# Five weight places and three key places in a two-layer kernel, with a 4 KB descriptor area

## The reference

```python
def peer(h, wq, subkeys, u_tab, v_tab):
    t = h.reshape(-1, D_MODEL)
    q = (t @ wq).reshape(-1, PEER_HEADS, 2, PEER_QDIM // 2)
    s = jnp.einsum('thpd,hpkd->thpk', q, subkeys)
    sv, si = lax.top_k(s, PEER_TOPK)
    cand = sv[:, :, 0, :, None] + sv[:, :, 1, None, :]
    cv, ci = lax.top_k(cand.reshape(*cand.shape[:2], 256), PEER_TOPK)
    idx = i1 * PEER_KEYS + i2          # the two halves' keys of ci
    g = softmax(cv)
    act = gelu(einsum('td,thkd->thk', t, u_tab[idx]))
    out = einsum('thk,thkd->td', g * act, v_tab[idx])
```

## Time and profile before

| what | value |
|---|---|
| time, median of 3 runs | 2362.88 us (2361.84 to 2364.53) |
| profiled execution: span from its first to its last instruction | 2360.1 us |
| that execution's own time | its span is all that is given; the median stands 2.8 us above it |
| opening, to the first gather | 0 to 176.0 us |
| stages 0 and 1, gathers 0 to 511 | 176.0 to 1586.3 us |
| gap, to gather 512 | 1586.3 to 1664.2 us |
| stage 2, to the last landing and the output | 1664.2 to 2360.1 us |
| DMA, mean over the span | 398 GB/s, 939.43 MB |

### The profile page before, as it was taken

One profiled execution on the slowest core, in us unless ns is written; L12 is line 12 of the kernel. 1 busy time (PEld: TensorE's weight loads), 2 busy tenths in 40 slices (PEclk: granted clock), 3 DMA queues, 4 the chain that ended last, 5 costly groups with the idle time before them and its releaser, 6 DMA issues.

```text
span 2360.1 us, 24134 instructions
## 1 busy us (share of the span) xinstructions
PE 2079.7 (88%) x6896; PEld 1123.8 (48%) x6896; DVE 1609.6 (68%) x3952; ACT 953.4 (40%) x2791; POOL 1019.5 (43%) x868
## 2 busy tenths in 40 slices
PE   8998998899998988988898998798899988777787
PEld 7775554455564434544454544346455533222222
DVE  3855668967766568788866677855765887666454
ACT  2014434543334444444454333534543444444333
POOL 0004444344334444444444454530333555566774
PEclk9999999999999999999999999999999999999999
DMA  9979999999999999999999999996799999999997
GB/s 400 375 291 382 395 399 421 407 421 421 421 420 421 415 421 404 421 421 417 391 421 421 421 421 421 416 370 254 284 365 379 415 421 421 422 421 421 422 421 318
DMA packets 132595, 939.43 MB, mean 398 GB/s; under 512 B 14720, under 2 KB 17920, under 8 KB 18944
## 3 DMA queue, kind: packets, MB, share of 16 engines
q0 software_dynamic: 110592, 805.36, 82.8%
q1 hardware_dynamic: 21888, 132.68, 13.8%
HBM read 936.93 MB, written 1.05 MB: 397 GB/s over the span
## 4 chain that ended last, share of the span: by engine, by line
PE 36%; DMA 33%; DVE 13%; issue 7%; POOL 6%; ACT 5%; POOLq 0%; SPq 0%; DVEq 0%; ACTq 0%
DMA uv<-uv_dram,stage_idx 31%; PE psum L983 19%; PE psum L786 9%; DVE uv L1593 6%; POOL uv L1050 5%; PE psum L768 4%; PE psum L926 1%; DMA uv<-in_dram 1%; ACT diag L1225 1%; DMA uv<-ada_dram 1%; ACT wv L1223 1%; DVE h L1282 1%; PE psum L704 1%; PE psum L957 1%; ACT gel L1221 1%
## 5 line engine op out<-in xcount | busy, mean ns | idle before, releaser
L983 PE MATMUL psum<-uv,diag 128*128 128x512 f32 x3072 | 1447.1, 611 | 227.8 <-ACT diag L1225 217.6
L1050 POOL DMA_INDIRECT uv<-uv_dram,stage_idx x768 | 985.9, 1284 | 1052.3 <-PE psum L983 829.5
L1593 DVE CUSTOM_DVE_ANT_0 uv<-uv,h 128x1024 f32<-128x1024 f32 x768 | 935.1, 1226 | 554.6 <-DMA uv<-uv_dram,stage_idx 545.2
L983 PEld LDWEIGHTS psum<-uv,diag 128*128 128x128 f32 x3072 | 562.1, 192 | 1006.5 <-issue 505.3
L1221 ACT ACTIVATE gel<-dots 128x1 f32<-128x1 f32 x768 | 155.3, 202 | 1060.6 <-DVE dots L1593 1059.7
L1225 ACT ACTIVATE diag<-const,wv 128x128 f32<-128x128 f32 x768 | 308.3, 401 | 25.0
L786 PE MATMUL psum<-hT,wring 128*128 128x256 f32 (+1 forms) x1312 | 273.0, 361 | 0.7 <-ACT hT L1091 0.7
L786 PEld LDWEIGHTS psum<-hT,wring 128*128 128x128 f32 x1312 | 233.1, 190 | 60.2 <-issue 33.0
L1223 ACT ACTIVATE wv<-gel,gw 128x1 f32<-128x1 f32 x768 | 226.3, 295 | 25.0
L1038 POOL COPY stage_idx<-idx 128x8 uint32 (+1 forms) x96 | 33.4, 348 | 265.4 <-DVE idx L1564 264.7
L1073 ACT ACTIVATE work<-psum 128x256 f32<-128x256 f32 (+2 forms) x123 | 47.7, 389 | 128.5 <-PE psum L786 102.1
(11 more groups left out here) (224 smaller groups left out, 1289.8 us busy)
## 6 DMA issues: line engine op xcount, KB each, us to landing
uv<-ada_dram SPq DMA_DIRECT2D x30, 1024.0 KB, 15.8
wring<-in_dram SPq DMA_DIRECT2D x25, 1024.0 KB, 9.5
wring<-wq_dram SPq DMA_DIRECT2D x24, 1024.0 KB, 11.2
uv<-uv_dram,stage_idx POOLq DMA_INDIRECT x768, 14.2
uv<-in_dram SPq DMA_DIRECT2D x9, 1024.0 KB, 13.5
uv<-ada_t_dram SPq DMA_DIRECT2D x7, 1024.0 KB, 22.7
wring<-ada_dram SPq DMA_DIRECT2D x6, 1024.0 KB, 11.2
wring<-ada_t_dram SPq DMA_DIRECT2D x5, 1024.0 KB, 20.7
```

What stands on the lines that cost most here:

```text
L983: last = mm(acc[:, b, :], diag[:, s % RING, :], uv[:, s % RING, D + 512 * b:D + 512 * (b + 1)], start=(c == 0), stop=(c == NSEL - 1))
L1050: nc.gpsimd.indirect_dma_start(out=uv[:, s, :], out_offset=None, in_=tables[stage // 2], in_offset=bass.IndirectOffsetOnAxis(ap=stage_idx[ ...
L1593: v.tensor_tensor_reduce(out=uv[:, r, 0:D], in0=uv[:, r, 0:D], in1=h2[:, row_of[stage], t, :], scale=1.0, scalar=0.0, op0=ALU.mult, op1=AL ...
```

## The change

`WRING` goes from 3 to 5 and the keys' places from 2 to 3 (`KEYS`). The room comes from a smaller area in which GpSimd keeps the descriptors of its DMAs (`dynamic_dma_scratch_size=4096`), from 6 places for the diagonal matrices instead of 8 (`DIAGS`; ACT now waits until PE has used the one six slots back), from `sp_t` laid over the end of `xn`, and from small tiles packed into one. Gap blocks get `uv` slots alone, unless they are used beyond the gap's search, when they get own places. The `out_w` blocks of the opening may lie in `uv` slots 2 to 7 instead of 4 to 7. Head 1's query weights of stage 2 are loaded once. Keys are loaded one query block later than before, except for a stage's first three heads and at its end.

```diff
-WRING = 3
+WRING = 5
-LAST_SLOTS = (4, 5, 6, 7)
+LAST_SLOTS = (2, 3, 4, 5, 6, 7)
 RING = 8
+DIAGS = 6
 LAG = 2
+SCRATCH = 4096
+KEYS = 3
...
-            uses = [(("query", *args[:2], args[3] if reloaded(*args[:2]) else 0), ("wq", args[0] // 2, args[1]))]
+            uses = [(("query", *args[:2], 0), ("wq", args[0] // 2, args[1]))]
...
-    own, opening, gap = list(range(WRING)), list(range(WRING + RING)), list(range(WRING)) + [WRING + i for i in GAP_SLOTS]
+    own, opening, gap = list(range(WRING)), list(range(WRING + RING)), [WRING + i for i in GAP_SLOTS]
...
-        keys = sb("keys", [P, 2, SUB_W])
+        keys = sb("keys", [P, KEYS, SUB_W])
...
-        diag = sb("diag", [P, RING, P])
+        diag = sb("diag", [P, DIAGS, P])
...
+        sp_t = view(work, 2 * D - P, P)
...
-                pe.wait_ge(keys_landed[h % 2], 16 * (stage * PH // 2 + h // 2 + 1))
+                pe.wait_ge(keys_landed[(k - 1) % KEYS], 16 * ((k - 1) // KEYS + 1))
...
-                    last = mm(acc[:, b, :], diag[:, s % RING, :], uv[:, s % RING, D + 512 * b:D + 512 * (b + 1)],
+                    last = mm(acc[:, b, :], diag[:, s % DIAGS, :], uv[:, s % RING, D + 512 * b:D + 512 * (b + 1)],
...
+            def load_keys(layer):
+
+                nonlocal heads
+                heads += 1
+                if heads > KEYS:
+                    sp.wait_ge(*scored[heads - KEYS])
+                sp.dma_start(keys[:, (heads - 1) % KEYS, :], A["keys"][layer, (heads - 1) % PH])\
+                    .then_inc(keys_landed[(heads - 1) % KEYS], 16)
...
-                if kind == "wq" and b == heads % PH:
-                    heads += 1
-                    if heads > 2:
-                        sp.wait_ge(*scored[heads - 2])
-                    sp.dma_start(keys[:, b % 2, :], A["keys"][layer, b]).then_inc(keys_landed[b % 2], 16)
+                if kind == "wq":
+                    queries += 1
+                    while heads < queries and (heads < queries - 1 or queries % PH <= KEYS):
+                        load_keys(layer)
...
-                f(diag[:, r, :], C("ident"), ACT.Copy, scale=wv[:, r:r + 1]).then_inc(diag_ready, 1)
+                if s >= DIAGS:
+                    act.wait_ge(uv_used, RING + s - DIAGS + 1)
+                f(diag[:, s % DIAGS, :], C("ident"), ACT.Copy, scale=wv[:, r:r + 1]).then_inc(diag_ready, 1)
...
-    nc = bacc.Bacc("TRN2", target_bir_lowering=False, num_devices=1)
+    nc = bacc.Bacc("TRN2", target_bir_lowering=False, num_devices=1, dynamic_dma_scratch_size=SCRATCH)
```

More of the change, by code:

```diff
@@ L339, in weight_blocks @@
     return list(blocks.values())
-def reloaded(stage, h):
-    return stage == 2 and h == 1
 def weight_places(program, blocks):
-    own, opening, gap = list(range(WRING)), list(range(WRING + RING)), list(range(WRING)) + [WRING + i for i in GAP_SLOTS]
+    own, opening, gap = list(range(WRING)), list(range(WRING + RING)), [WRING + i for i in GAP_SLOTS]
     found = program.index(("step", ("find", 2, 0, (0,), FIND_PARTS - 1)))
@@ L397, in build @@
         wring = sb("wring", [P, WRING, BLK_W])
-        keys = sb("keys", [P, 2, SUB_W])
+        keys = sb("keys", [P, KEYS, SUB_W])
         hT = sb("hT", [P, KC, TOK])
         h2 = sb("h2", [P, 2, TT, D])
[L402 to L406, removed]
+        small = sb("small", [P, 9 * 2 + 3 * HEADS + 3 * RING + 8])
+        ss_x, ms_x, rr_x, ss_v, ms_v, rr_v, lam_dot, lam_exp, neg_lam = (small[:, 2 * i:2 * i + 2] for i in range(9))
+        ss_o, ms_o, rr_o = (small[:, 18 + HEADS * i:18 + HEADS * (i + 1)] for i in range(3))
+        dots, gel, wv = (small[:, 30 + RING * i:30 + RING * (i + 1)] for i in range(3))
+        unused = small[:, 30 + 3 * RING:38 + 3 * RING]
         ss_heads, ms_heads, root_heads = (sb(s, [P, 16]) for s in ("ss_heads", "ms_heads", "root_heads"))
@@ L416, in build @@
         stage_idx = sb("stage_idx", [P, 2, RING], U32)
-        dots, gel, wv = (sb(s, [P, RING]) for s in ("dots", "gel", "wv"))
         work = sb("work", [P, 8704])
@@ L536, in build @@
         w_landed = [sem(f"w_landed{i}") for i in range(WRING + RING)]
-        keys_landed = [sem(f"keys_landed{i}") for i in range(2)]
+        keys_landed = [sem(f"keys_landed{i}") for i in range(KEYS)]
         act_bank_full, act_took = sem("act_bank_full"), sem("act_took")
@@ L942, in query @@
             def query(stage, h, q, tiles):
-                again = reloaded(stage, h)
-                channel_major(to_act, ("query", h), q, tiles, again or tiles[0] == 0, again or tiles[-1] == TT - 1)
+                channel_major(to_act, ("query", h), q, tiles, tiles[0] == 0, tiles[-1] == TT - 1)
                 n["qh", stage, h] = to_act.n
@@ L956, in score @@
                         o = (q * len(tiles) + i) * P
-                        last = mm(bank[:, o:o + P], qh[:, h % 2, q, t * P:(t + 1) * P], keys[:, h % 2, q * PK:(q + 1) * PK],
+                        last = mm(bank[:, o:o + P], qh[:, h % 2, q, t * P:(t + 1) * P], keys[:, (k - 1) % KEYS, q * PK:(q + 1) * PK],
                                   start=True, stop=True)
@@ L994, in _ @@
             sp.dma_start(const[:, 0:W_EARLY], A["const"][:, 0:W_EARLY]).then_inc(const_loaded, 16)
-            heads = 0
+            heads = queries = 0
+            def load_keys(layer):
[5 more added lines that the diff above has]
+                    .then_inc(keys_landed[(heads - 1) % KEYS], 16)
             for n, (kind, layer, b, _, _) in enumerate(blocks):
```

## The result

The changed kernel takes 2367.42 us, the median of 18 runs (2365.58 to 2373.24), against 2363.18 for the kernel before, 18 runs beside it (2358.95 to 2367.21). The medians differ by 4.2 us. The ratio of the runs is 1.0024, with a 95% interval of 1.0016 to 1.0031: slower by about 5.7 us (3.8 to 7.3). The forecast was 2363.7, in a range of 2354.5 to 2371.0.

The account below looks back on a forecast made before the run. DMA traffic of gathers and weights (421 GB/s) bounds full stretches, PE close behind or leading elsewhere. Terms −5.0 + 1.0 + 4.3 + 1.5 + 0 − 1.0 = +0.8 on 2360.1, plus 2.8 from span to median: 2363.7 us, range 2354.5 to 2371.

Parts of the forecast that it names:

- the rival in which PE takes the saving over: Stage 1: PE, 5% behind DMA, becomes the bound, so the −5.0 us becomes 0; 2368.7 us, chance 0.16.
- gains and losses cancel: Whole kernel: the forecast itself, terms summing to +0.8 us, own range 2358 to 2368, chance 0.44.
- Two loads leave stage 1: Stages 0 and 1: two weight loads fewer in the full stretches, 2.49 us each, −5.0 us (0 to −7.5).
- full-stretch gathers 5 us ahead at 1586: End of stage 1: sign that the forecast is right, gathers landing 5 us earlier at 1586 us.
- Start of the gap: First gap load waits for uv slot 7, +4.3 us; lower granted clock after PE's longer idling, +1.5 us.
- Start of stage 0: Gather into slot 2 waits for PE's out_w matmuls, others queue behind it on POOL; +1.0 us (0 to +2.0).
- slots 6 and 7 go out at 196.67 as before: Start of stage 0: gathers into these slots keep their issue time, since PE's next 16 matmuls end at 195.84.
- The keys of the last head: Stage 2: keys issued at 1815.07 us, just ahead of full last slices, come earlier; −1.0 us (−0.3 to −4.2).
- the rival of two more transfers there: Stage 2: removed and earlier loads give back two transfers (−5.0), gap clock stays up (−1.5); 2357.2 us, chance 0.32.
- What was costed at nothing: Six diagonals on ACT, 0 (+0.5 at most), and keys in three places one query block later, 0.
- The descriptor area: POOL's gathers: with 4 KB, late issues from gather 28, then every 21, 36 instead of 7, about 3 us each; cost 0.
- The rival of up to +87 us: Full descriptor area keeps POOL back until the queue runs dry; up to +87 us, 2451, chance 0.08.

Follow-up runs that it names:

- the kernel of rising order: Changed kernel with the gap's weight blocks taking uv slots in rising order (2, 3, 4 ...) instead of falling; 2362.50 us, 1.0004 of before.
- filler: Changed kernel with 31 instead of 10 filler products on PE ahead of the gap's first modulation block; 2365.01 us, 1.0017 of before.

## Why the prediction was right or wrong

The measured 2367.42 us lies in the range and 3.7 us above the forecast, but that is in part luck: a term of +5.0 us was missing, and the range reached up to 2371 for another reason, the rival in which PE takes the saving over. That gains and losses cancel is only nearly so. By the median the time lies just within the forecast's own line of 0.2% (2367.6), by the ratio of 1.0024 just beyond it, and the interval (1.0016 to 1.0031) leaves out 1.

**Two loads leave stage 1: right.** −5.0 was forecast, −4.8 is what the landings between gathers 424 and 448 show; between traces with `uv` at a like multiple (32, 128, or 256 and more) it is −4.9 to −5.0. The sign "full-stretch gathers 5 us ahead at 1586" did not come, because the slower pace had used the gain up: gather 504 lands 0.2 us earlier than before. The rival in which PE takes the saving over is refuted: its time, 2368.7, is the nearest of the rivals' to the measured 2367.42, but its mechanism did not happen.

**Start of the gap: right in mechanism, near in size.** +4.3 for the late load and +1.5 for the clock were forecast. From L702 to L766, 1600.30 to 1607.43 us, it is 7.1 us, against 4.9 in the kernel of rising order: +2.2 for the clock. The wait grew from 1.70 to 5.40 us: +3.7, and "PE's wait for it near 6 us" is 5.40. Together +5.9 for +5.8. The run of rising order shows that both come from the order of places: 4.9 us by the medians. With `uv` at a multiple of 256 the same edit makes 0.9883 of 0.9894, 2.6 us, with overlapping intervals.

**Start of stage 0: a step wrong, the size not resolved.** The waits came as forecast, but the step "slots 6 and 7 go out at 196.67 as before" failed: they went out at 192.10 and after, since PE's last matmuls on `out_w` ended at 190.98 and not at 195.84. The +1.0 is not refuted by that: from the issue of gather 0, gather 24 lands 1.1 us later in the middle of the traces, within their scatter.

**The keys of the last head: not seen.** Gather 512 is issued 8.0 us later than before and gather 584 8.4, so the −1.0 did not show in stage 2's first gathers. Nor did the rival of two more transfers there.

**What was costed at nothing.** ACT stands nowhere ahead of the diagonal matrices (L1233) for a free place, and PE waits for no keys, in the changed kernel's trace: both zeros hold.

**The descriptor area: right that it costs nothing, right in how often it acts, wrong in how long.** A first late issue at gather 28, then every 21, 36 in all, was forecast and is what the traces show. Each was put at 3.0 us and is 0.60. The rival of up to +87 us is refuted by 1.0003; with 36 x 0.60 = 21.6 us in place of 7 x 2.58 = 18.1 us of late issue, POOL had hardly more to make up than before.

**What was missing: the place of uv.** The prediction costed the diagonals and the keys by their waits and did not cost the packing of small tiles at all: it did not ask where they put the tiles behind them. The kernel before shifted by 32 bytes costs 2367.71 − 2362.66 = +5.0 us by the medians. The sum as measured is −4.8 + 3.7 + 2.2 + 5.0 = +6.1 us, or +7.2 with the unresolved 1.1 of stage 0's start, and the ratio says 5.7 (3.8 to 7.3). The forecast of +0.8 had the first terms nearly right and not the last one. With `uv` at a multiple of 32 in both, the changed kernel and the shifted kernel before stand at the same ratio, 1.0024.

The Trainium skill has a rule that bears on it: "DMA: Bandwidth & Descriptors", section "How a descriptor splits into AXI transactions", says that when a descriptor does not start 256B-aligned, "its first transaction starts at the 256 B boundary below the descriptor's start", and that the bytes before the start still cost. For a row of 8 KB that makes 33 transactions in place of 32, an estimate from that page. The runs agree on the 256: 2.445 us there, 2.483 to 2.492 elsewhere, which is 1.6% to 1.9% longer and not the 3.1% of one transaction in 32. No run here shows the transactions. Nor do the runs agree with a cost that goes with the bytes ahead: starts of 32 and of 224 past a multiple of 256 both gave 2.492, and starts of 128 and of 192 both about 2.485.

What stays open: 2.3 us in the last seven gathers of stage 1 in the changed kernel's trace, which the kernels of rising order and of filler do not show at that size (0.1 and 1.0), but the kernel before shifted by 32 bytes does (2.5), so that it is not the change's alone; and some 2 us by which gather 0 starts at another time in executions whose opening is the same (174.85 us in the changed kernel, 172.78 in that of rising order). The worth of the change with the gap repaired, at a like place of `uv`, is resolved in one pair: 0.9967 (0.9955 to 0.9980) against 0.9995 (0.9986 to 1.0004) at a multiple of 128, some 6.6 us less, though `wring` moved there too. At 32 it is 1.0004 (0.9995 to 1.0013) against 1.0024 (1.0011 to 1.0038), 4.7 us less with intervals that just overlap. At 256 and more the times show nothing, 0.9883 against 0.9884, where −5 us would be 0.9979 of it, although the traces have the step of 4.9 us between gathers 424 and 448 there too.

## What to carry to other kernels

A DMA share of 1.0 does not say that a transfer is as short as it can be: compare the pace of equal transfers between two kernels, to the third digit, and look where their destination begins. A change that moves tiles changes that, whatever else it does; put the tile that most bytes are written to at a multiple of 256 and the packed small tiles behind it. And where one more place is given, ask in which order the places are taken: here the first load got the place that came free last. A forecast of how often something happens and one of how long it lasts are two forecasts; read both from the trace.

## What the runs showed of the hardware that was not expected

A gather of 128 rows of 8 KB into `uv` landed every 2.492 us at a start that is a multiple of 32 alone, every 2.483 to 2.487 at 64 and 128, and every 2.445 at 256 and beyond, worth 27 us of 2362 in the kernel before, by one tile of 64 bytes. A descriptor area of 4 KB turned 7 late issues of 2.58 us, every 106 gathers, into 36 of 0.60 us, every 21, without a change in time. And 5.40 us without work on PE were followed by 32 matmuls at a granted clock of 0.50, in 3.64 us; with 62 filler matmuls ahead of them (7.08 us) and 0.68 us left to wait they took 1.93 us.
